# Attention weights transposed one step later, convolution taps moved beside the linear attention's values, and a scan's few-row products spread between matmuls

## The chip, the core and the metric

The kernel runs on one core of a Trainium2 chip. Five engines work side by side, each on its own in-order list of instructions, and meet at semaphores: TensorE (PE) for matrix products, VectorE (DVE), ScalarE (ACT), GpSimd (POOL), and SyncE (SP), which here issues the transfers of weights. The metric is the time of one execution in microseconds (us).

## What is computed

Two transformer blocks over 512 positions of width 1024, in float32. Only the parts that the change touches are shown.

```python
# block 1: three branches, gated, merged, then a feed-forward network
y_a = mla_branch(...)   # 8 heads, low-rank queries and keys, softmax attention
y_b = fox_branch(...)   # 8 heads, softmax attention with decay
y_c = ssm_branch(...)   # 16 heads, chunked state scan
# attention, by blocks of 128 queries
s = einsum('bqhd,bkhd->bhqk', q, k) * scale + mask
out = einsum('bhqk,bkhd->bqhd', softmax(s), v)
# block 2: spatial gating, gated linear attention, band attention (8 heads,
# with a bias), and a depthwise convolution of 31 taps with a layer norm
log_a = log_sigmoid(a_lr @ w_a2 + b_a) / 16
cum = cumsum(log_a)                      # in chunks of 64
k_dec = k * exp(total - cum); state = exp(total) * state + k_dec.T @ v
y = silu(layer_norm(depthwise_conv(glu, w[31])))
```

## The kernel before

**Precision.** A float32 product is made of three passes of a fast form: every operand is split into a high and a low part, and `product` (L393 to L395) issues high*high, low*high, high*low. A matmul of 128x128 by 512 columns appears on PE as one record.

**Weights.** All weights come as "slabs" of up to 1 MB through three buffers. For each slab SyncE issues the transfer, ScalarE writes its high part (`split`, L1124), VectorE the low part (`split`, L1623), and PE waits for that in `slab`. Where these two splits stand in the lists of ScalarE and VectorE is written by hand: `split(i)` makes all slabs up to number i. A slab of a gate (`gate_slab`) holds 256 output columns: two halves of 24 matmuls each, or four quarters of 12.

**Order.** The program is a list of stages (mla, fox, ssm, ..., convin, band, sgu, gla, gates2, ...). Four engines meet at the end of a stage (`boundary`); PE only reports there and goes on.

**Softmax attention** (`attention`, three times: tags mla, fox, band) runs over 16 steps, step j being one pair of heads and one block of queries t = j % 4, with t+1 blocks of keys. In a step PE makes the scores of both heads (L487), VectorE adds the mask and takes the row's bound (L1751), ScalarE takes the exponential in place and its sum (L1177), VectorE takes a reciprocal for each head (L1762) and scales the weights (L1763), PE transposes them (L498), ScalarE copies each head's transpose out of PSUM (L1188), PE multiplies them with the values (L511). PE transposes step j-2 (`LAG_T`) and multiplies step j-3 (`LAG_O`) behind the scores of step j; VectorE scales step j-1 behind the scores of step j. The first transposes of a stage have four extra matmuls before them (`keep_clock`, L388). In mla VectorE also splits one slab, right behind score 16.

**Scan** (`pe_ssm`, four tiles t of 128 positions). Few-row products `arow(q)` (L660) spread a row of running sums over the partitions: 16 rows of the array, four heads each. Between them stand the state products (L670, L677), the diagonal products (L688), transposes of finished rows (`yturn`, L643), and nine gate slabs (`SCAN_GATES`), two in each t and one behind. VectorE turns an `arow` into differences (`diff`, L2013), ScalarE into exponentials (`decay`, L1325), VectorE mixes them (`mix`, L2023), and the diagonal products wait for that.

**Depthwise convolution.** It is 124 "taps" on VectorE, each one instruction over 128x512 (L2338): 16 in convin, 60 beside the band's slabs, 8 inside the band's attention (one for every fourth score), 24 beside the slabs of sgu, and the last 16 at the end of sgu, ahead of the split for the slab "gasm". Behind them PE sums over channels (`column_sums`, L926: "cmean", later "cvar").

**Linear attention** (`pe_gla`). PE: slab gasm, cmean, two products with 16 rows ("la", L811, after a transfer of `gla_w_a2_2` that ScalarE issues at the stage's start, L1456), the values gv (two slabs), keys gqk 2 and 3, cvar, queries gqk 0 and 1, transposes of keys, gr. ScalarE makes the softplus of "la" in three steps and only then the high part of gv's second slab. VectorE then:

```python
split(slab_of["gasm", 0] + 1)
dve_conv_mean()
split(slab_of["gv", 0, 0])      # waits for ScalarE's high part
dve.wait_ge(soft_ready, 3)      # then softplus, and 16 cumulative scans
```

**Start of mla.** After the second of six low-rank columns both engines split slab 1 and VectorE builds the position tables (`dve_tables`), ScalarE their sines; the split of slab 2 comes behind.

## Time and profile before

| | us |
|---|---|
| median of 3 runs (2138.02 to 2139.4) | 2138.96 |
| the profiled execution | 2145.03 |
| its span on the core | 2143.3 |
| PE busy in the span | 2063.6 |
| VectorE busy | 1148.3 |
| ScalarE busy | 797.4 |

PE is busy for 96% of the span. The profiled execution is 6.07 us longer than the median run, 1.73 us of that outside its span. The trace lists, for each instruction, when it started, how long it took, and what ended the idle time before it. "PEclk" is the granted clock of TensorE: 1.00 is 2.4 GHz, 0.50 is 1.2 GHz.

### The profile page before, as it was taken

How to read it: one execution, taken by the hardware profiler on the slowest of the kernel's cores; microseconds unless marked ns; L12 is line 12 of the kernel's file. 1: busy time of each engine (PE TensorE's matmuls, PEld its weight loads, DVE VectorE, ACT ScalarE, POOL GpSimd, SP SyncE). 2: the span in 40 equal slices, each digit the busy share in tenths (PEclk: the TensorE clock that was granted, in tenths of full speed). 3: DMA queues.
4: the chain of work that ended last, by engine and by line, in shares of the span. 5: the costliest groups of instructions: out<-in, count | busy, mean ns of one | idle time of the engine just before them, and what ended most of it. 6: DMA issues, size and time to landing. Idle time of an engine off the chain costs nothing.

```text
span 2143.3 us, 23661 instructions
## 1 busy us (share of the span) xinstructions
PE 2063.6 (96%) x9677; PEld 1679.8 (78%) x9677; DVE 1148.3 (54%) x1706; ACT 797.4 (37%) x1116; POOL 28.3 (1%) x54
## 2 busy tenths in 40 slices
PE   7999999999999999999999899999999999999985
PEld 5886688878888788888878587888888788888874
DVE  5746637566434666366368884543435443234245
ACT  5536643344422433133232635342233333133132
POOL 0000000110000000000000000000000000000000
PEclk9999999999999999999999999999999999999998
DMA  4320023211333232332333122133232233333221
GB/s 126 99 79 21 1 79 99 79 59 59 118 99 98 79 99 98 98 93 84 100 117 99 41 89 79 59 99 99 98 97 86 76 97 98 98 99 98 98 90 58
DMA packets 164442, 184.45 MB, mean 86 GB/s; under 512 B 6759, under 2 KB 125798, under 8 KB 164334
## 3 DMA queue, kind: packets, MB, share of 16 engines
q1 hardware_dynamic: 160718, 173.98, 25.7%
q10 hardware_dynamic: 2912, 6.83, 0.9%
q0 software_dynamic: 704, 2.13, 0.3%
q8 instruction: 77, 1.26, 0.2%
q14 instruction: 31, 0.25, 0.0%
HBM read 180.81 MB, written 2.12 MB: 85 GB/s over the span
## 4 chain that ended last, share of the span: by engine, by line
PE 90%; DVE 6%; ACT 2%; issue 1%; DMA 0%; SPq 0%; POOL 0%; DVEq 0%; ACTq 0%; POOLq 0%
PE ps L393 27%; PE ps L395 26%; PE ps L394 26%; PE ps L487 2%; PE ps L511 1%; PE ps L498 1%; PE ps L468 1%; ACT arena L1149 1%; DVE WL L1623 1%; PE ps L660 1%; PE ps L688 1%; DVE arena L2338 1%; DVE arena L1713 0%; PE ps L670 0%; DVE X L2147 0%
## 5 line engine op out<-in xcount | busy, mean ns | idle before, releaser
L1623 DVE TENSOR_TENSOR WL<-W,WH 128x2048 fp32r<-128x2048 f32 (+1 forms) x166 | 375.4, 2261 | 382.6 <-ACT WH L1124 374.7
L393 PE MATMUL ps<-HH,WH 128*128 128x512 f32 x1400 | 550.1, 393 | 9.0 <-DVE HL L1646 4.6
L395 PE MATMUL ps<-HH,WL 128*128 128x512 f32 x1400 | 546.2, 390 | 0.0
L394 PE MATMUL ps<-HL,WH 128*128 128x512 f32 x1400 | 546.1, 390 | 0.0
L1124 ACT ACTIVATE WH<-W 128x2048 fp32r<-128x2048 f32 (+1 forms) x166 | 313.2, 1888 | 291.3 <-DMA W<-in_w_ff_dram 117.6
L393 PEld LDWEIGHTS ps<-HH,WH 128*128 128x128 f32 x1400 | 263.4, 188 | 67.5 <-issue 6.6
L395 PEld LDWEIGHTS ps<-HH,WL 128*128 128x128 f32 x1400 | 263.6, 188 | 55.3
L394 PEld LDWEIGHTS ps<-HL,WH 128*128 128x128 f32 x1400 | 263.7, 188 | 54.5 <-issue 0.7
L393 PE MATMUL ps<-WH,arena_r 128*128 128x512 f32 (+1 forms) x616 | 239.6, 389 | 2.8 <-issue 2.8
L395 PE MATMUL ps<-WH,arena_r 128*128 128x512 f32 (+1 forms) x616 | 239.2, 388 | 0.0
L394 PE MATMUL ps<-WL,arena_r 128*128 128x512 f32 (+1 forms) x616 | 239.0, 388 | 0.0
L393 PE MATMUL ps<-WH,HH 128*128 128x512 f32 x352 | 140.4, 399 | 5.6 <-DVE HL L1646 3.1
L394 PE MATMUL ps<-WL,HH 128*128 128x512 f32 x352 | 139.0, 395 | 0.0
L395 PE MATMUL ps<-WH,HL 128*128 128x512 f32 x352 | 139.0, 395 | 0.0
L393 PEld LDWEIGHTS ps<-WH,arena_r 128*128 128x128 f32 x616 | 116.2, 189 | 28.1 <-issue 5.2
L394 PEld LDWEIGHTS ps<-WL,arena_r 128*128 128x128 f32 x616 | 116.1, 189 | 23.1
L395 PEld LDWEIGHTS ps<-WH,arena_r 128*128 128x128 f32 x616 | 116.1, 188 | 23.0
L1384 ACT ACTIVATE arena<-ps,par 128x512 f32<-128x512 f32 x56 | 38.6, 689 | 209.1 <-PE ps L395 209.0
L2147 DVE TENSOR_TENSOR X<-X,ps 128x512 f32<-128x512 f32 x48 | 32.9, 685 | 100.2 <-PE ps L395 100.2
L393 PEld LDWEIGHTS ps<-WH,HH 128*128 128x128 f32 x352 | 67.4, 191 | 22.1 <-issue 8.3
L1435 ACT ACTIVATE arena<-ps 128x512 f32<-128x512 f32 x44 | 26.4, 599 | 155.4 <-PE ps L395 152.6
L2338 DVE SCALAR_TENSOR_TENSOR arena<-arena,par 128x512 f32<-128x512 f32 x120 | 81.1, 743 | 0.3 <-POOLq L1017 0.3
(328 smaller groups left out, 2257.6 us busy)
## 6 DMA issues: line engine op xcount, KB each, us to landing
W<-in_w_in_dram SPq DMA_DIRECT2D x50, 1024.0 KB, 5.1
W<-in_w_ff_dram SPq DMA_DIRECT2D x32, 1024.0 KB, 5.2
W<-in_ffn_w_up_dram SPq DMA_DIRECT2D x44, 512.0 KB, 4.6
W<-in_w_gate_dram SPq DMA_DIRECT2D x16, 1024.0 KB, 5.0
W<-in_ffn_w_down_dram SPq DMA_DIRECT2D x10, 1024.0 KB, 5.0
W<-in_w_out_dram SPq DMA_DIRECT2D x8, 1024.0 KB, 5.0
W<-in_w_branch_dram SPq DMA_DIRECT2D x8, 1024.0 KB, 5.0
W<-in_w_br_ssm_dram SPq DMA_DIRECT2D x4, 1024.0 KB, 5.0
```

The costliest lines, as they stand in the source:

```text
L393: pe.matmul(out_, st[0], mv[0], start=first, stop=False)
L394: pe.matmul(out_, st[0], mv[1], start=False, stop=False)
L395: return pe.matmul(out_, st[1], mv[0], start=False, stop=last)
L468: tr = pe.transpose(banks[k][:, t * P:(t + 1) * P], at(XN, NT, DM)[:, t, k * P:(k + 1) * P], ident[:, :])
L487: pe.matmul(b[:, 0:n], lhs(2 * pair + odd, t), rhs(2 * pair + odd, n), start=True, stop=True).then_inc(pe_done, 1)
L498: tr = pe.transpose(b[:, kb * P:(kb + 1) * P], p[:, r % 6, kb * P:(kb + 1) * P], ident[:, :])
L1124: act.activation(WH[:, j % RING, 0:n], W[:, j % RING, 0:n], ACT.Copy).then_inc(slab_hi, 1)
L1384: freed(act.activation(gate_tile(tag, i, c), b[:, :], ACT.Sigmoid, bias=pcol(bname, n * KT + cc * 4 + c)), ((tag, "g", n, cc), c))
L1435: freed(act.activation(raw[:, i % 2, c, 2:2 + S], b[:, :], ACT.Copy), (("up", i), c))
L1623: dve.tensor_tensor(WL[:, j % RING, 0:n], W[:, j % RING, 0:n], plain(WH[:, j % RING, 0:n]), ALU.subtract).then_inc(slab_lo, 1)
L2147: freed(dve.tensor_tensor(X[:, t, sl], X[:, t, sl], b[:, :], ALU.add), (tag, t, half))
L2338: ins = dve.scalar_tensor_tensor(y[:, c, :], glu[:, c, j:j + S], w, y[:, c, :], ALU.mult, ALU.add)
```

## The change

Six edits are made together.

1. `attention`, all three: `LAG_T` 2 to 3 and `LAG_O` 3 to 4. The weights lie in a buffer with a place for each t (`weights`), so they may live four steps. One reciprocal serves both heads, once both exponentials are there. For t of 0 and 1 both heads' transposes go to one bank and are copied at once.
2. Scan: `arow(0)` and `arow(1)` moved behind the state products, `arow(1)` between the halves of the gate slab; `arow(3)` and `yturn` between the halves of the second gate slab. VectorE's and ScalarE's lists follow.
3. Taps: none inside the band's attention, none at the end of sgu; 24 remain for gla, 8 of them right behind the split of gv's second slab, 16 behind the cumulative scans.
4. gla on PE: cmean behind gv instead of behind gasm, cvar behind both gqk slabs; VectorE's and ScalarE's parts of the convolution's norm follow. `cum` and `ke` move to other memory, since the taps' input still lives in the old place.
5. The transfer of `gla_w_a2_2` is issued at the start of sgu, with a semaphore of its own (`decay_in`).
6. Start of mla: slab 2 is split together with slab 1, before the tables.

The diff, with lines that only rename buffers left out:

```diff
@@ -48,7 +48,7 @@
     NB = 8
-    LAG_T, LAG_O = 2, 3
+    LAG_T, LAG_O = 3, 4
     PAIR_BANKS = (6, 7)
@@ -278,6 +279,22 @@
+def turned(s):
+    return s - s % 2 if s // 2 % NT < 2 else s
+def weights(p, s):
+    t = s // 2 % NT
+    at0 = t * (t + 1) * P + s % 2 * (t + 1) * P
+    return p[:, at0:at0 + (t + 1) * P]
+def turned_weights(pts, s):
+    n = (s // 2 % NT + 1) * P
+    at0 = s // 2 % 2 * 2 * S + s % 2 * n
+    return pts[:, at0:at0 + n]
@@ -322,7 +339,7 @@
 TAP_ORDER += [(j, c) for j in range(FIRST_TAPS, TAPS) for c in range(4)]
-TAPS_SLAB = 10
+TAPS_SLAB, LAST_TAPS = 10, 16
 BIAS = 14336
@@ -394,7 +411,7 @@
-    def gemm_f(name, w, kt, c0, tiles, src, n0=0):
+    def gemm_f(name, w, kt, c0, tiles, src, n0=0, between=None):
@@ -402,6 +419,8 @@
             mm.then_inc(pe_done, 1)
+            if between is not None and c == tiles // 2 - 1:
+                between()
@@ -490,27 +509,31 @@
                 for r in (2 * i, 2 * i + 1):
-                    b = bank((tag, "PT", r))
+                    if turned(r) == r:
+                        b, c = bank((tag, "PT", r)), 0
                     if r == 0:
...
                     for kb in range(t + 1):
-                        tr = pe.transpose(b[:, kb * P:(kb + 1) * P], p[:, r % 6, kb * P:(kb + 1) * P],
-                                          ident[:, :])
-                    tr.then_inc(pe_done, 1)
+                        tr = pe.transpose(b[:, (c + kb) * P:(c + kb + 1) * P],
+                                          weights(p, r)[:, kb * P:(kb + 1) * P], ident[:, :])
+                    c = t + 1
+                    if r == 2 * i + 1 or t >= 2:
+                        tr.then_inc(pe_done, 1)
             i = j - LAG_O
...
                     o = bank((tag, "O", pair), counted=False, pinned=PAIR_BANKS[pair % 2])
-                taken(pe, (tag, "PT", 2 * i))
-                taken(pe, (tag, "PT", 2 * i + 1))
+                taken(pe, (tag, "PT", turned(2 * i + 1)))
+                if t >= 2:
+                    taken(pe, (tag, "PT", 2 * i))
                 for kb in range(t + 1):
...
                                        v[:, kb, h * HD:(h + 1) * HD],
-                                       pts[:, (2 * i + odd) % 4, kb * P:(kb + 1) * P],
+                                       turned_weights(pts, 2 * i + odd)[:, kb * P:(kb + 1) * P],
                                        start=(kb == 0), stop=(kb == t))
@@ -661,8 +684,6 @@
-            arow(0)
-            arow(1)
             if t > 0:
@@ -676,8 +697,9 @@
                               start=True, stop=True).then_inc(pe_done, 1)
+            arow(0)
             for n, kind, cc, j in SCAN_GATES[2 * t]:
-                gate_slab("G1", n, kind, cc, j)
+                gate_slab("G1", n, kind, cc, j, lambda: arow(1))
             pe.wait_ge(xdt_ready, t + 1)
@@ -693,21 +715,23 @@
                     arow(2)
-                    arow(3)
+                    def small_products():
+                        arow(3)
+                        if t > 0:
+                            yturn(t - 1)
                     for n, kind, cc, j in SCAN_GATES[2 * t + 1]:
-                        gate_slab("G1", n, kind, cc, j)
-                    if t > 0:
-                        yturn(t - 1)
+                        gate_slab("G1", n, kind, cc, j, small_products)
         for n, kind, cc, j in SCAN_GATES[2 * NT]:
...
-    def gate_slab(tag, n, kind, cc, j):
+    def gate_slab(tag, n, kind, cc, j, between=None):
...
             w = slab(KT, 256, gate(2 * cc + j))
-            gemm_f((tag, "g", n, cc), w, KT, 0, 2, hn, 2 * j)
+            gemm_f((tag, "g", n, cc), w, KT, 0, 2, hn, 2 * j, between)
             slab_read()
@@ -716,10 +740,10 @@
             w = slab(kt, 512, krc(br, cc))
-            gemm_f((tag, "b", n, cc), w, kt, 0, 4, lambda k: [yh[:, k, :], yl[:, k, :]])
+            gemm_f((tag, "b", n, cc), w, kt, 0, 4, lambda k: [yh[:, k, :], yl[:, k, :]], 0, between)
         else:
             w = slab(kt, 256, krc(br, 2 * cc + j, 256))
-            gemm_f((tag, "b", n, cc), w, kt, 0, 2, lambda k: [yh[:, k, :], yl[:, k, :]], 2 * j)
+            gemm_f((tag, "b", n, cc), w, kt, 0, 2, lambda k: [yh[:, k, :], yl[:, k, :]], 2 * j, between)
         slab_read()
@@ -794,31 +818,31 @@
                   lambda h, n: KT_[part(h), h // 2, 0:n],
-                  at(12288, NT, 512), at(18432, 6, S), at(0, 4, S))
+                  at(12288, NT, 512), at(18432, 2560), at(0, 4 * S))
...
         slab_read()
-        pe.wait_ge(dve_taps, 4 * TAPS)
-        column_sums("cmean", at(CONV, 4, S))
         wa2, alr = at(25344, 256), at(22528, S)
-        pe.wait_ge(load_in, 16 * 5)
+        pe.wait_ge(decay_in, 16)
         taken(pe, ("gasm", 0))
...
         gemm_t_long("gv", full, 1536, hnt)
+        pe.wait_ge(dve_taps, 4 * TAPS)
+        column_sums("cmean", at(CONV, 4, S))
         w = slab(KT, 256, win(1280, 1536, "w_in_2"))
...
         slab_read()
-        pe.wait_ge(conv_squared, 4)
-        column_sums("cvar", at(18432, 4, S))
         w = slab(KT, 256, win(1024, 1280, "w_in_2"))
...
         slab_read()
+        pe.wait_ge(conv_squared, 4)
+        column_sums("cvar", at(18432, 4, S))
@@ -1171,21 +1195,25 @@
             if j < N // 2:
-                n = (j % NT + 1) * P
                 for s in (2 * j, 2 * j + 1):
                     taken(act, (tag, "S", s))
-                    act.activation(p[:, s % 6, 0:n], p[:, s % 6, 0:n], ACT.Exp, bias=rowneg[:, s:s + 1],
+                    act.activation(weights(p, s), weights(p, s), ACT.Exp, bias=rowneg[:, s:s + 1],
                                    scale=-1.0, accum_out=rowsum[:, s:s + 1]).then_inc(probs_ready, 1)
...
                 n = (i % NT + 1) * P
-                for r in (2 * i, 2 * i + 1):
-                    b = use(act, (tag, "PT", r))
-                    if i >= 2:
-                        act.wait_ge(pairs_out, N // 2 * nth + i - 1)
-                    freed(act.activation(pts[:, r % 4, 0:n], b[:, 0:n], ACT.Copy), (tag, "PT", r))
+                if i >= 2:
+                    act.wait_ge(pairs_out, N // 2 * nth + i - 1)
+                if i % NT < 2:
+                    b = use(act, (tag, "PT", 2 * i))
+                    both = pts[:, i % 2 * 2 * S:i % 2 * 2 * S + 2 * n]
+                    freed(act.activation(both, b[:, 0:2 * n], ACT.Copy), (tag, "PT", 2 * i))
+                else:
+                    for r in (2 * i, 2 * i + 1):
+                        b = use(act, (tag, "PT", r))
+                        freed(act.activation(turned_weights(pts, r), b[:, 0:n], ACT.Copy), (tag, "PT", r))
@@ -1200,7 +1228,7 @@
             if i == 1:
-                split(slab_of["c", 2])
+                split(slab_of["c", 2] + 1)
                 act.wait_ge(cos_arg, 1)
@@ -1338,9 +1366,9 @@
             decay(4 * t)
-            decay(4 * t + 1)
             if t > 0:
                 scale(t - 1)
+            decay(4 * t + 1)
             for n, kind, cc, j in SCAN_GATES[2 * t]:
@@ -1450,10 +1478,9 @@
             freed(act.activation(V[:, t, :], b[:, :], ACT.Copy), ("av", t, 0))
-        attention("band", 2, at(18432, 6, S), at(0, 4, S))
+        attention("band", 2, at(18432, 2560), at(0, 4 * S))
     def act_gla():
-        act.dma_start(at(25344, 256)[0:16, :], A["gla_w_a2_2"][0]).then_inc(load_in, 16)
         b = result(("gasm", 0))
@@ -1465,13 +1492,12 @@
         act.activation(la, la, ACT.Ln, bias=1.0).then_inc(soft_ready, 1)
+        v, r = at(14336, NT, 512), at(12288, NT, 512)
         split(slab_of["gv", 0, 0])
-        act_conv_squares()
-        v, r = at(14336, NT, 512), at(12288, NT, 512)
         for t in range(NT):
...
             freed(act.activation(v[:, t, :], b[:, :], ACT.Copy), ("gv", t, 0))
-        cum, ke = at(22528, 2, S), at(23552, 2, S)
+        cum, ke = at(2048, 2, S), at(3072, 2, S)
         act.wait_ge(decay_sums_ready, 1)
@@ -1479,22 +1505,22 @@
                        ACT.Exp).then_inc(decay_exps_ready, 1)
+        act_conv_squares()
         qz, kd = at(8192, 4, S), at(10240, 2, S)
...
             freed(act.activation(kd[:, c, :], b[:, :], ACT.Copy), ("gqk", 2 + c))
-        split(slab_of["gqk", 0] + 1)
-        taken(act, "cvar")
-        act.activation(at(11776, S), at(11776, S), ACT.Sqrt).then_inc(conv_root_ready, 1)
         for c in range(2):
...
             freed(ins, ("gqk", c))
+        split(slab_of["gr", 0, 0])
+        taken(act, "cvar")
+        act.activation(at(11776, S), at(11776, S), ACT.Sqrt).then_inc(conv_root_ready, 1)
         act_conv_out()
-        split(slab_of["gr", 0, 0])
         for t in range(NT):
@@ -1518,6 +1544,7 @@
     def act_sgu():
+        act.dma_start(at(25344, 256)[0:16, :], A["gla_w_a2_2"][0]).then_inc(decay_in, 16)
         act.dma_start(at(12288, 4, P), A["sg_w_2"][0].rearrange("g i j -> i g j")).then_inc(load_in, 16)
@@ -1746,9 +1773,9 @@
                     b = use(dve, (tag, "S", s))
-                    if s >= 6:
-                        use(dve, (tag, "PT", s - 6))
-                    freed(dve.tensor_tensor_reduce(out=p[:, s % 6, 0:n], in0=b[:, 0:n],
+                    if s >= 8:
+                        use(dve, (tag, "PT", turned(s - 8)))
+                    freed(dve.tensor_tensor_reduce(out=weights(p, s), in0=b[:, 0:n],
                                                    in1=mask(2 * pair + s % 2)[:, S - n:S],
@@ -1756,11 +1783,10 @@
             if 0 <= i < N // 2:
-                n = (i % NT + 1) * P
+                dve.wait_ge(probs_ready, base + 2 * i + 2)
+                link(dve.reciprocal(rowinv[:, 2 * i:2 * i + 2], rowsum[:, 2 * i:2 * i + 2]))
                 for s in (2 * i, 2 * i + 1):
-                    dve.wait_ge(probs_ready, base + s + 1)
-                    link(dve.reciprocal(rowinv[:, s:s + 1], rowsum[:, s:s + 1]))
-                    dve.tensor_scalar(p[:, s % 6, 0:n], p[:, s % 6, 0:n], rowinv[:, s:s + 1], None, ALU.mult)\
+                    dve.tensor_scalar(weights(p, s), weights(p, s), rowinv[:, s:s + 1], None, ALU.mult)\
                         .then_inc(weights_ready, 1)
@@ -1807,7 +1833,7 @@
             if i == 1:
-                split(slab_of["c", 2])
+                split(slab_of["c", 2] + 1)
                 dve_tables()
@@ -2026,7 +2052,6 @@
             diff(0)
-            diff(1)
             if t > 0:
@@ -2055,12 +2080,13 @@
             mix(0)
+            diff(1)
             mix(1)
...
             diff(2)
+            mix(2)
             diff(3)
-            mix(2)
             mix(3)
@@ -2188,17 +2214,13 @@
-        def beside_scores(s):
-            if s % 4 == 3:
-                taps(1)
-        attention("band", 2, at(18432, 6, S), lambda h: bias[:, h, :], at(4096, 4, S), beside_scores)
+        attention("band", 2, at(18432, 2560), lambda h: bias[:, h, :], at(4096, 4, S))
...
         dve.tensor_scalar(stat2[:, 0:2], pcol("gla_b", 0, 2), -1.0, None, ALU.mult).then_inc(gate_bias_ready, 1)
-        lv, la, cum, ke = at(20480, 2, S), at(21504, 2, S), at(22528, 2, S), at(23552, 2, S)
-        split(slab_of["gasm", 0] + 1)
-        dve_conv_mean()
+        lv, la, cum, ke = at(20480, 2, S), at(21504, 2, S), at(2048, 2, S), at(3072, 2, S)
         split(slab_of["gv", 0, 0])
+        taps(len(TAP_ORDER) - tapped[0] - LAST_TAPS)
         dve.wait_ge(soft_ready, 3)
@@ -2208,6 +2230,9 @@
         ins.then_inc(decay_sums_ready, 1)
+        taps(LAST_TAPS)
+        split(slab_of["gqk", 2])
+        dve_conv_mean()
         split(slab_of["gqk", 2] + 1)
@@ -2215,8 +2240,6 @@
         split(slab_of["gqk", 0] + 1)
-        dve_conv_norm()
-        split(slab_of["gr", 0, 0])
         kz = at(16384, NT, 2, 256)
@@ -2225,6 +2248,8 @@
             freed(ins, ("kd", c))
+        split(slab_of["gr", 0, 0])
+        dve_conv_norm()
         split(slab_of["gr", 0, 0] + 1)
@@ -2291,7 +2316,6 @@
         dve.tensor_tensor(v, v, bc(bb.unsqueeze(1), [P, NT, 512]), ALU.add).then_inc(sgu_values_ready, 1)
-        taps(len(TAP_ORDER) - tapped[0])
         split(slab_of["su", 3] + 1)
```

## Rows read from the trace of the kernel before

**Rows 1.** The page: the chain that ended last, by engine.

```profile
PE 90%; DVE 6%; ACT 2%; issue 1%; DMA 0%; SPq 0%; POOL 0%; DVEq 0%; ACTq 0%; POOLq 0%
```

**Rows 2.** Waits of PE: line, waited for, us in total, times, longest.

```profile
PE ps L498 <- DVE arena L1763: 8.7, 9, 1.7
...
PE ps L811 <- DMA arena<-in_gla_w_a_dram: 2.4, 1, 2.4
```

**Rows 3.** Timeline of ScalarE and PE, start of mla: start, us, instruction, [idle before].

```profile
42.21 1.90 ACT L1124 ACTIVATE WH<-W 128x2048 fp32r<-128x2048 f32 x1
...
46.55 0.50 PE L393 MATMUL ps<-HH,WH 128*128 128x512 f32 x1 [2.03 <-DVE WL L1623]
```

**Rows 4.** Windows: length, busy by engine, granted clock; scan five, then mla, band, gla.

```profile
437.50:440.90 3.40, 3.40 (x5) 1.35 (x4) 3.40 (x13) 3.34 (x6) 1.90 (x1) 0.50 0.02 5
...
512.60:515.90 3.30, 3.30 (x6) 1.45 (x5) 3.27 (x6) 1.50 (x3) 0.33 (x1) 0.50 0.00 0
185.00:188.20 3.20, 3.20 (x15) 2.06 (x14) 0.82 (x4) 1.51 (x5) 0.00 (x0) 0.50 0.01 3
1229.70:1232.90 3.20, 3.20 (x20) 2.49 (x19) 1.65 (x5) 1.06 (x3) 0.00 (x0) 0.52 0.00 0
1297.80:1304.40 6.60, 6.60 (x15) 4.34 (x14) 0.00 (x0) 5.80 (x6) 0.00 (x0) 0.50 0.00 0
```

**Rows 5.** Timeline of VectorE and PE, mla attention.

```profile
180.40 2.28 DVE L1623 TENSOR_TENSOR WL<-W,WH 128x2048 fp32r<-128x2048 f32 x1
...
183.64 1.22 PE L498 MATMUL ps<-ident,arena 128*128 128x128 f32 x8 [1.65 <-DVE arena L1763]
...
203.80 1.05 PE L498 MATMUL ps<-ident,arena 128*128 128x128 f32 x6 [0.61 <-DVE arena L1763]
```

**Rows 6.** Band attention: one pair's window, PE's waits, two of VectorE's groups.

```profile
1206.80:1216.95 10.15, 8.84 (x79) 5.39 (x78) 9.06 (x36) 7.37 (x24) 0.00 (x0) 1.00 0.00 0
...
PE ps L498 <- DVE arena L1763: 5.7, 5, 1.7
...
L2338 DVE SCALAR_TENSOR_TENSOR arena<-arena,par 128x512 f32<-128x512 f32 x6 | 4.5, 748 | 0.0
L1762 DVE RECIPROCAL rowinv<-rowsum 128x1 f32<-128x1 f32 x24 | 3.8, 156 | 0.0
```

**Rows 7.** Timeline of PE and VectorE in the scan, t = 2.

```profile
472.83 2.04 PE L660 MATMUL ps<-arena,ident 16*128 16x128 f32 x16
...
484.95 2.29 DVE L1623 TENSOR_TENSOR WL<-W,WH 128x2048 fp32r<-128x2048 f32 x1
493.96 2.16 DVE L2013 TENSOR_SCALAR arena<-ps,arena 128x128 f32<-128x128 f32 x8 [6.71 <-PE ps L660]
```

**Rows 8.** Timeline of VectorE and ScalarE, sgu's end and gla's start.

```profile
1272.85 10.69 DVE L2338 SCALAR_TENSOR_TENSOR arena<-arena,par 128x512 f32<-128x512 f32 x16
...
1305.43 1.90 ACT L1124 ACTIVATE WH<-W 128x2048 fp32r<-128x2048 f32 x1
...
1307.36 2.29 DVE L1623 TENSOR_TENSOR WL<-W,WH 128x2048 fp32r<-128x2048 f32 x1 [10.10 <-ACT WH L1124]
1309.57 1.22 DVE L2203 SCALAR_TENSOR_TENSOR arena<-arena 128x1024 f32<-128x1024 f32 x1
...
1311.55 3.02 DVE L2208 TENSOR_TENSOR_SCAN arena<-ones,arena 128x64 f32<-128x64 f32 x16
```

**Rows 9.** Timeline of PE in the same stretch, to the first transposed keys' use.

```profile
1284.72 0.50 PE L393 MATMUL ps<-HH,WH 128*128 128x512 f32 x1 [1.35 <-DVE WL L1623]
1290.34 3.59 PE L926 MATMUL ps<-arena,ones 128*128 128x512 f32 x8
1296.38 2.59 PE L811 MATMUL ps<-arena 16*128 16x512 f32 x4 [2.45 <-DMA arena<-in_gla_w_a_dram]
...
1323.37 0.39 PE L393 MATMUL ps<-HH,WH 128*128 128x512 f32 x1
...
1361.13 3.72 PE L839 MATMUL ps<-arena 128*128 128x256 f32 x16 [0.59 <-DVE arena L2226]
```

17 lines of the change are left out of this document (9 added, 8 removed).

## The prediction

> **What bounds the kernel now.** I read the page first. PE carries 90% of the chain that ended last, VectorE 6%, ScalarE 2% [rows 1]. So the time is PE's list of work, plus the places where PE waits, plus the stretches in which its matmuls run at half clock. An edit that only frees VectorE or ScalarE is worth what PE waits for them and no more.
>
> Second, the table of PE's waits. The one that the attention edit aims at is PE waiting for VectorE's scaled weights, 8.7 us in nine waits; the transfer that edit 5 aims at costs 2.4 us [rows 2]. Third, the granted clock in short windows. It fell to 0.50 (1.2 GHz) in five stretches of the scan, although PE is busy in all of each, in one stretch of the mla attention, in one near the end of the band attention, and for 6.6 us in gla [rows 4]. Work in a stretch of x us at half clock would take x/2 at full clock, so a stretch of 3.3 us costs about 1.65 us. Last, timelines of each place that the change touches.
>
> **Start of mla (edit 6).** PE waits 2.03 us for VectorE's low part of slab 2, whose high part ScalarE makes only at 42.21, behind the sine [rows 3]. The edit puts both splits ahead of the tables, where PE has two column tiles (24 matmuls each, which take 5.6 us in gasm [rows 9]) before it needs the slab. The tables move back by one split (2.29 us) plus a wait for ScalarE; nothing on PE waits for them here. Worth -2.0; bounds 0 (if the late tables delay the column sums behind them) and -2.0.
>
> **Attention (edit 1).** PE has the same matmuls. What changes is how long the weights of a step have: one whole step more, 2.6 us on average (a pair of heads, four steps, takes 10.15 us in band [rows 6]). Per pair VectorE has four reciprocals of 0.16 us fewer, ScalarE two copies fewer.
>
> - fox: PE is unbroken except for a wait of 0.61 us at the end, as in mla, where the row is 203.80 [rows 5], because the last weights are needed at once. Behind the last scores PE now has more left to do. -0.5.
> - mla: the same 0.61, and 1.65 us behind the slab that VectorE splits between two scores (2.28 us) [rows 5]. Then PE ran at half clock for 3.2 us, worth 1.6 [rows 4]. The extra step covers the late weights. But ScalarE's exponential of the next score waits for the same split, and ScalarE's copies are queued behind that exponential; so PE meets the lateness one step later, at the multiplication with the values. I take half of the wait away (-0.8) and half of the clock's cost (-0.8), since in band 1.3 us without PE work in a pair left the clock at 1.00 [rows 6] and one of 1.65 here did not. With the tail -2.2; bounds -0.6 and -3.9.
> - band: five waits, 5.7 us in all, for weights [rows 6]. They recur once a pair, after the longest step, where a tap of 0.75 us and two reciprocals stand between the score and the weights. Both causes go. The last wait is followed by a half-clock stretch of 3.2 us (0.52), worth 1.5 [rows 4]. New waits: at the start PE reaches its first multiplication having made four scores, and ScalarE's copy stands behind eight exponentials; I add 1.2 there, and 0.5 for copies in the rest. Sum -5.7 - 1.5 + 1.7 = -5.5; bounds -3 (the clock stays low, copies cost another 1 us) and -7.
>
> **Scan (edit 2).** No instruction is added or removed on PE. Its eight runs of 16 records of few-row matmuls (L660) take 2.04 us each; the timeline has each of the five half-clock stretches beginning within 1 us of the end of one, as the run that ends at 474.9 [rows 7]. Three runs had none behind them. The change cuts each run into two of 1.0 us with 5.6 us of dense work between them. Other work there (diagonal products, transposes) also fills the attentions, where the clock stayed up through unbroken pairs. So I expect the stretches to go: 16.6 us at 0.50 are worth 8.3. I leave one of the five, since a 16-row run now touches eight transposes, and take -6.8; bounds 0 and -8.3.
>
> What could eat it is VectorE's order. Now `diff(1)` comes behind the state updates, `mix(1)` behind that, and the split of the next gate slab behind `mix(1)`. Counting from the end of the last diagonal products at t = 2, with durations of this trace: rows' end, 3.6; `diff(0)` at 5.3 to 6.4; output and state updates (eight of 0.7) to 12; `mix(0)`, `diff(1)`, ScalarE's exponential, `mix(1)` to 15.1; ScalarE's high part to 16.3, the low part (2.29 [rows 7]) to 18.6. PE asks for the slab at 19.8. Slack 1.2 us; at t = 3 the same count leaves 0.3. I put the loss at 0.
>
> **sgu and gla (edits 3 to 5).** Four costs go:
> - 16 taps of 0.67 us no longer stand before the split of gasm's slab: the 1.35 us wait goes [rows 8, 9].
> - The 2.45 us wait for the transfer goes [rows 9]; in its place PE waits about 0.7 us for ScalarE's copy of gasm, which cmean used to cover.
> - The half-clock stretch of 6.6 us behind that wait [rows 4]: "la" has only 16 rows, so I let half of it stay (in "la" and the start of gv, where it does not delay VectorE and so is lost in the wait below).
> - The 0.59 us wait for the copies of transposed keys [rows 9].
>
> One cost comes, and it is the largest: PE now stands at cmean, behind gv, until the last tap. When is that? sgu ends on VectorE when its four outputs are done, some 3.8 us earlier than before; gasm's matmuls start at 1283.4 (1284.72 - 1.35) and end at 1289.0, "la" starts at 1289.65 instead of 1296.38 [rows 9], 6.7 us earlier. All that hangs on "la" moves with it. ScalarE's high part of gv's second slab, before at 1305.43 to 1307.3, ends at 1300.6; VectorE idled 10.10 us for it before [rows 8] and idles nearly as long after, because the taps stand behind that split, not before it. Then VectorE has: low part 2.29 (to 1302.9), 8 taps 5.35 (to 1308.2), softplus and scans 5.0 (from 1309.57 to 1314.57 before [rows 8]; to 1313.2), 16 taps 10.69 (to 1323.9). PE starts gv 2.6 us behind "la", at 1292.25. Before, gv took from 1298.97 to 1323.37, 24.4 us, with 5.4 us of it at half clock, so 21.7 at full; it would end at 1314.0. It idles 9.9 us. The work that it would hide under is at the front: VectorE's idle 10 us.
>
> Then cmean 3.6, and half clock after a wait this long, for 2 us of loss (the one after 2.45 us of waiting lasted 6.6 us, worth 3.3 [rows 4]). So the first gqk matmul comes at 1323.9 + 3.6 + 2.0 = 1329.5, against 1323.37 before [rows 9]: +6.1. Behind it cvar and the norm have more time than before, and -0.6 for the keys' copies: +5.5. Bounds +3 (no half clock, and the chain of "la" 0.8 us quicker) and +8.
>
> Here a rule of the Trainium skill was weighed. The trace shows half clock in the scan with no idle time on PE. The Trainium skill ("TensorE: Matmul & The Clock Gate", section "HAM oscillation") blames idle gaps of the matrix engine for the loss of clock; by that the scan's stretches are not the few-row products' doing, and the edit would bring nothing there. The trace disagrees in that there was no gap. The same page (section "Part 4: PE-mode transpose") says that transposes do not count as busy; by that a run of `arow(3)` with `yturn` is as bad as before. The attentions, nearly a third of whose work is transposes, kept the clock up here.
>
> **The sum**: -2.0 - 2.2 - 0.5 - 5.5 - 6.8 + 5.5 = -11.5 us. The profiled execution took 2145.03, 6.07 above the median of the runs. The differences are taken over to the median: 2138.96 - 11.5 = **2127.5**.
>
> **The rivals.**
> - *The clock in the scan does not come back* (it falls around any group of small products, wherever it stands). For: PE was busy there throughout, so no idle gap explains it. Against: the runs of 2.04 us beside the stretches. +6.8: 2134.3. The Trainium skill's rule on idle gaps, above, would give this.
> - *The extra lag brings nothing*: PE waits for ScalarE's copies instead of VectorE's weights, once a pair. For: ScalarE's list in a step is serial, exponentials first. Against: it is busy 7.37 of 10.15 us a pair in band [rows 6]. Band and mla give up their 7.7: 2135.2.
> - *The taps hide after all*: VectorE is done before gv ends. It would need 10 us more before the split. +5.5 becomes about -6.4: 2115.6. Only a list that runs otherwise than I read would do this.
> - *Slower: the gate slabs come late.* If VectorE's chain in the scan is longer than counted and each of seven gate slabs in the loop finds its low part a whole split (2.29 us) late, PE loses 16.0: 2143.5. It decides from 1.7 us a slab on (11.5 / 7), that is 2.9 us beyond my count at t = 2. Speaking for it: VectorE waits for `arow(1)` in the middle; against: the count has no item that I could not read.
>
> **How the numbers follow.** The forecast (2121 to 2132) 0.60; the clock does not return 0.13; the lag brings nothing 0.10; taps hide 0.05; late slabs 0.08; the rest, several small misses, 0.04. The best of all bounds together is -2.0 - 3.9 - 0.6 - 7 - 8.3 + 3 = -18.8, or 2120.2; the range goes a little below it for the hidden taps, and above to the two rivals at 2134 to 2135 with some 2 us: 2118 to 2137. A difference under 0.2% (4.3 us) is no more than a measurement of this kernel can tell from none. Faster means under 2134.7, slower over 2143.2: the forecast, the taps, and half of the two middle rivals (0.60 + 0.05 + 0.12, and 0.01 of the rest) give 0.78 faster; 0.14 the same; 0.08 slower.
>
> **What would show it.** In the profile after: no wait of PE near 46.5; no wait for weights in band, some 1 us for copies at its start; the clock at 1.00 through the scan in all but one place; no wait before gasm or for a transfer; one wait of PE at the column sums behind gv, 8 to 10.5 us, released by a tap, and VectorE idle for some 9 us ahead of gv's second low part. The prediction is wrong if that wait is missing or doubled by clock, if the scan has waits for low parts, or if half clock stays around its small products.

## The result, and the profile after

The changed kernel takes **2127.53 us** (median of nine runs, 2126.11 to 2135.53), beside 2138.83 for the kernel before in the same session: a ratio of 0.9944, 95% interval 0.9929 to 0.9959, that is -12.0 us (-8.8 to -15.2). The forecast was 2127.5.

The profiled execution took 2127.42 us with a span of 2125.7; that of before took 2145.03. So the two traces differ by 17.6 us and the medians by 11.3, and the first task is to see which part of the 17.6 belongs to the change. Windows between the same instructions of both kernels tell. First the kernel before, in the stretches of mla attention, scan, and band to sgu's first transposes, and then of everything from gla's end to the embedding's first transposes, where nothing was changed (columns as in [rows 4]):

```profile
160.84:208.87 48.03, 44.78 (x309) 29.46 (x308) 33.71 (x133) 34.40 (x100) 0.00 (x0) 0.96 0.07 23
402.65:556.20 153.55, 153.55 (x761) 124.46 (x759) 98.50 (x165) 67.14 (x74) 9.97 (x5) 0.94 0.20 62
1191.26:1257.40 66.14, 59.80 (x405) 41.58 (x406) 56.73 (x166) 37.78 (x103) 0.00 (x0) 0.97 0.16 49
1405.07:2087.76 682.69, 671.08 (x2962) 555.26 (x2961) 267.41 (x271) 207.44 (x226) 0.00 (x0) 0.99 0.29 95
```

The same stretches of the changed kernel, then its two half-clock places (band, gla), which answer to [rows 4]:

```profile
156.74:201.68 44.94, 41.42 (x310) 28.69 (x309) 31.38 (x117) 33.74 (x92) 0.00 (x0) 1.00 0.08 25
393.46:542.00 148.54, 148.54 (x761) 119.64 (x759) 97.03 (x165) 67.28 (x74) 9.48 (x5) 1.00 0.20 64
1176.06:1238.37 62.31, 58.34 (x404) 41.60 (x405) 49.08 (x142) 36.92 (x95) 0.00 (x0) 0.97 0.17 52
1391.45:2070.48 679.03, 667.02 (x2961) 551.96 (x2960) 267.31 (x271) 207.52 (x226) 0.00 (x0) 0.99 0.30 96
...
1183.50:1187.00 3.50, 3.50 (x22) 2.21 (x18) 1.93 (x9) 2.33 (x9) 0.00 (x0) 0.54 0.01 2
1299.50:1309.80 10.30, 5.17 (x7) 2.24 (x8) 7.27 (x9) 1.59 (x8) 0.00 (x0) 0.51 0.01 2
```

The fourth row of each is the lesson in reading a single pair of traces: the same instructions, no edit, and 3.7 us less, because in this execution less time at half clock followed the waits of the norms there, 6.8 us of it where before had 17.1. By the starts of the same instructions on PE, the stretches that the change touches and the rest come to:

| stretch (us on PE) | before | after | difference | forecast |
|---|---|---|---|---|
| start of mla, the wait alone | 2.03 | 0 | -2.0 | -2.0 |
| mla attention | 48.03 | 44.94 | -3.1 | -2.2 |
| fox attention, to the sums behind z | 90.6 | 88.6 | -2.0 | -0.5 |
| scan | 153.55 | 148.54 | -5.0 | -6.8 |
| band attention and its end | 66.14 | 62.31 | -3.8 | -5.5 |
| sgu and gla, to the updates | 103.7 | 109.3 | +5.5 | +5.5 |
| all changed stretches | | | -10.4 | -11.5 |
| everything else (half clock that fell otherwise) | | | -7.2 | 0 |

-10.4 for the changed stretches agrees with the medians' -11.3. The last row need not be the change's doing: in the fourteen profiled kernels of this document, the stretch from gla's end to the embedding takes 677.2 to 682.9 us with the same instructions, with 3.4 to 17.1 us of half clock, and both ends of that range come from kernels with all six edits. In the table of PE's waits of the changed kernel, what answers to [rows 2] is this; L518 stands where L498 stood, L534 is the multiplication with the values:

```profile
PE ps L950 <- DVE arena L2362: 9.5, 1, 9.5
...
PE ps L534 <- ACT arena L1212: 6.2, 8, 2.1
...
PE ps L410 <- DVE WL L1650: 1.5, 1, 1.5
```

The 8.7 us for VectorE's scaled weights are gone and 6.2 us for ScalarE's copies have come; the 2.4 us for the transfer and the waits for low parts ahead of slab 2 of mla and of gasm are gone; and one wait of 9.5 us for a tap has come, at cmean (L950). PE's share of the chain that ended last went from 90% [rows 1] to 91%, ScalarE's from 2% to 3%:

```profile
PE 91%; DVE 5%; ACT 3%; issue 1%; DMA 0%; SPq 0%; POOL 0%; DVEq 0%; POOLq 0%
```

The band attention in the timeline of PE, the rows with a wait; they answer to the waits of [rows 6]:

```profile
1183.16 0.63 PE L534 MATMUL ps<-arena 128*64 128x128 f32 x4 [2.06 <-ACT arena L1212]
1193.58 0.44 PE L534 MATMUL ps<-arena 128*64 128x128 f32 x4 [0.29 <-ACT arena L1212]
1202.48 0.44 PE L534 MATMUL ps<-arena 128*64 128x128 f32 x4 [0.30 <-ACT arena L1212]
1211.38 0.44 PE L534 MATMUL ps<-arena 128*64 128x128 f32 x4 [0.72 <-ACT arena L1212]
```

One step of the pipeline still ends late in every pair, but it is ScalarE's copy, queued behind exponentials. The largest comes at the start, and the half-clock window at 1183.5 above lies behind it.

And gla's start on VectorE and PE, which answers to [rows 8, 9]:

```profile
1281.47 2.29 DVE L1650 TENSOR_TENSOR WL<-W,WH 128x2048 fp32r<-128x2048 f32 x1 [9.59 <-ACT WH L1148]
1283.68 5.39 DVE L2362 SCALAR_TENSOR_TENSOR arena<-arena,par 128x512 f32<-128x512 f32 x8
...
1290.97 3.02 DVE L2230 TENSOR_TENSOR_SCAN arena<-ones,arena 128x64 f32<-128x64 f32 x16
1293.91 10.66 DVE L2362 SCALAR_TENSOR_TENSOR arena<-arena,par 128x512 f32<-128x512 f32 x16
...
1304.62 6.14 PE L950 MATMUL ps<-arena,ones 128*128 128x512 f32 x8 [9.53 <-DVE arena L2362]
1310.20 0.79 PE L410 MATMUL ps<-HH,WH 128*128 128x512 f32 x1
```

VectorE idles 9.59 us for ScalarE's high part, with 24 taps still to do, and a little later PE idles 9.53 us for the last of these taps.

### The profile page after: what moved, and what is told of

It reads as the page before. It is cut to its first block, busy times and chain, and to the rows that moved or that the text cites. A ratio compares the mean times of both kernels' runs of the same rounds, so it can differ in the third digit from the quotient of the medians.

```text
span 2125.7 us, 23510 instructions
## 1 busy us (share of the span) xinstructions
PE 2043.7 (96%) x9677; PEld 1666.8 (78%) x9677; DVE 1140.8 (54%) x1658; ACT 795.9 (37%) x1092; POOL 28.4 (1%) x54
## 4 chain that ended last, share of the span: by engine, by line
PE 91%; DVE 5%; ACT 3%; issue 1%; DMA 0%; SPq 0%; POOL 0%; DVEq 0%; POOLq 0%
PE ps L410 27%; PE ps L412 27%; PE ps L411 27%; PE ps L506 2%; PE ps L534 1%; PE ps L518 1%; ACT arena L1173 1%; PE ps L487 1%; PE ps L683 1%; DVE arena L2362 1%; PE ps L710 1%; DVE X L2173 0%; ACT arena L1200 0%; DVE arena L1740 0%; PE ps L950 0%
```

## Experiments

Every ratio is against the kernel before, run on the same chip in the same session. Length and clock of a stretch are from the one profiled execution of each kernel.

### One edit at a time

**Edit 2 alone** (scan), in the kernel before.

> The kernel before with edit 2 alone. Theory (the clock was lost behind the unbroken runs of 16 few-row matmuls, and putting dense matmuls between them has a price of its own): all five half-clock stretches of the scan go, worth 8.5 us, and the switching between small and dense matmuls gives 3.5 back, so the scan takes some 149 us instead of 154 and the kernel 2133.8 us (-5). Rival 1 (the stretches went for another reason, such as the other state of buffers and slabs that the rest of the change brings): stretches still there, switching paid for, 2142. Rival 2 (switching costs nothing and the 3.5 us came from elsewhere): 2130.3.

Measured: 2135.48 us, ratio 0.9971 (0.9955 to 0.9987), -6.2 us. The scan's window:

```profile
399.94:548.49 148.55, 148.55 (x761) 119.64 (x759) 97.09 (x165) 67.28 (x74) 9.48 (x5) 1.00 0.21 64
```

148.55 us at clock 1.00, to a hundredth what the changed kernel has. The edit does this by itself. Rivals 1 and 2 fall by the trace; the runs' interval alone (-2.8 to -9.6) would still hold rival 2.

**Edit 1 alone** (attention), the taps left inside band.

> The kernel before with edit 1 alone; the eight taps stay inside the band attention. Theory (the extra step of lag is what shortens the attentions): mla -3.1, fox -2.0, band -3 to -4 as in the changed kernel, 2130.5 us. Rival 1 (in band the gain needs the taps gone): band keeps about half of its waits for weights, 2132.5. Rival 2 (the lag brings nothing, and what mla and band gained came from the other edits): 2138.

Measured: 2129.66 us, ratio 0.9947 (0.9931 to 0.9962), -11.3 us. From band's first scores to sgu's first transposes, and the scan, which this kernel did not change:

```profile
1184.07:1245.41 61.34, 57.17 (x404) 40.72 (x405) 53.84 (x150) 37.24 (x95) 0.00 (x0) 1.00 0.17 52
```

```profile
393.38:551.50 158.12, 158.12 (x760) 128.01 (x759) 98.55 (x165) 67.12 (x74) 10.03 (x5) 0.91 0.19 60
```

mla took 44.94 as in the changed kernel, and band 61.34 at full clock, so edit 1 brings the gain with the taps in place; both rivals fall. No run separates its parts: the longer lag, the one reciprocal for two heads, and the one bank and copy for t of 0 and 1. The kernel with edits 1, 2 and 6 (`a_nogla`, below) has the taps in band and one half-clock stretch there and takes 62.85, against 62.31 of the changed kernel with one too: taking the taps out was worth 0.5 us. The scan is a second result: with the same instructions as in [rows 7], half clock came behind seven places here (27 us in all) instead of five, and took 4.6 us longer.

**Edits 3 to 5 undone**, in the changed kernel.

> The changed kernel with edits 3 to 5 undone: eight taps inside band's attention, the rest at the end of sgu, cmean behind gasm, the transfer in gla. Theory (these edits cost what the stretch from sgu's start to the updates lost): 2127.5 - 5.4 = 2122.1 us, less up to 1 that the taps cost in band. Rival (what they cost there comes back behind gla, by earlier low parts): 2127.5.

Measured: 2124.75 us, ratio 0.9926 (0.9910 to 0.9942), -15.8 against the kernel before, where the changed kernel has -12.0. Edits 3 to 5 cost some 4 us by the runs' ratios, whose intervals overlap, and 5.5 in the trace. The rival (what they cost comes back behind gla) falls by the traces alone. There the stretch from gla's end to the embedding took 682.86 us in this kernel and 679.03 in the changed one, but the difference goes with half clock (17.1 against 6.8 us) and not with the edits: `a_taps16` below, which has all of them, took 682.84.

**Edit 5 alone** (the transfer issued earlier), in the kernel before.

> The kernel before with edit 5 alone (the transfer of the decay's weights issued at the start of sgu). Theory 1 (the half clock behind la follows from PE's wait of 2.45 us for the transfer): the wait and the 6.8 us of half clock both go, -2.4 - 3.3 = -5.7 us of 2138.8: 2133.1. Theory 2 (the half clock follows from la's 16-row matmuls, as in the scan): only the wait goes, half clock stays, 2136.4. Rival (VectorE's low part of gv's second slab is what gv waits for in the end, so PE waits there instead): 2138.8.

Measured: 2136.55 us, ratio 0.9986 (0.9973 to 0.9999), -3.0 us, and in the profile no wait at la. Its stretch from la to the transposed keys:

```profile
1289.44:1338.48 49.04, 49.04 (x206) 38.28 (x206) 24.95 (x35) 28.36 (x43) 2.61 (x2) 1.00 0.23 74
```

49.04 us at clock 1.00, where the kernel before took 52.20 with 6.6 us at 0.50 [rows 4]. In this trace theory 1 holds: without PE's idle 2.45 us la's 16-row products were not followed by half clock. The runs' interval (-0.2 to -5.8) holds the -5.7 as its end only. The other profiles leave theory 2 open in part. All six kernels with the transfer in gla have half clock behind la, 3.4 to 6.8 us of it after a wait of 1.96 to 2.48 us. But of the seven in which PE waits only 0.8 us for the copy of gasm, four have it too, 3.4 us each (`a_copyfirst`, `a_best1`, `a_best2`, `a_best3`), and three have none (the changed kernel, `a_run16`, `a_taps16`). In `a_copyfirst` the granted clock is 0.50 from 1269.4 to 1272.8 us, right behind this:

```profile
1266.87 1.95 PE L833 MATMUL ps<-arena 16*128 16x512 f32 x4 [0.81 <-issue]
```

So the wait of 2 us is not the only condition there. `b_dma`, the one kernel without any half clock or wait there, has cmean directly ahead of la.

**Edit 6 alone** (slab 2 split ahead of the tables).

> The kernel before with edit 6 alone (slab 2 split ahead of the tables). Theory: PE's wait of 2.03 us for that low part goes and no other comes: from the first transposes to the mla attention 2.0 us less, apart from half clock. Rival (the late tables delay what stands behind them): a new wait of 0.5 to 2 us near 55 us for the column sums or the norm.

Run once, for the trace (2141.19 us): PE's waits between 30 and 60 us are only the 0.7 for ScalarE that stood there before, and the mla attention starts 2.3 us earlier. The late tables cost nothing. This kernel's mla attention happened to run at full clock:

```profile
158.53:204.94 46.41, 43.16 (x310) 28.50 (x309) 33.74 (x133) 34.34 (x100) 0.00 (x0) 1.00 0.07 24
```

46.41 against 48.03 is what half clock cost there (1.6), and 46.41 against 44.94 what edit 1 saves (1.5).

### The taps in VectorE's idle time

```diff
-TAPS_SLAB, LAST_TAPS = 10, 16
+TAPS_SLAB, LAST_TAPS = 10, 8
-                split(slab_of["gv", 0, 0])
                 taps(len(TAP_ORDER) - tapped[0] - LAST_TAPS)
+                split(slab_of["gv", 0, 0])
```

> The changed kernel with 16 of the 24 taps ahead of VectorE's low part of gv's second slab, and 8 behind the cumulative scans. Theory (VectorE stood idle for 9.6 us ahead of that low part and PE waited 9.5 us for the last tap, so the idle time takes the taps): the low part comes 1.1 us late at most, PE's wait at cmean shrinks to under 1 us, the half-clock stretch of 10 us behind it (worth 5) goes or shrinks to 3: 2127.5 - 9 - 4 = 2114.5 us. Rival 1 (the wait moves to gv's second slab, since the low part is then late by the taps): only 2 to 4 us gained, 2124. Rival 2 (the half clock has another cause, the 16-row matmuls of la): wait gone, half clock stays, 2118.5.

Measured: 2117.52 us, ratio 0.9888 (0.9872 to 0.9905). VectorE's timeline there, and the window from la to the transposed keys:

```profile
1269.45 10.69 DVE L2362 SCALAR_TENSOR_TENSOR arena<-arena,par 128x512 f32<-128x512 f32 x16
1280.77 2.29 DVE L1650 TENSOR_TENSOR WL<-W,WH 128x2048 fp32r<-128x2048 f32 x1 [0.62 <-ACT WH L1148]
...
1287.90 5.36 DVE L2362 SCALAR_TENSOR_TENSOR arena<-arena,par 128x512 f32<-128x512 f32 x8
```

```profile
1270.40:1322.83 52.43, 52.43 (x213) 39.77 (x213) 33.38 (x53) 29.62 (x45) 2.51 (x2) 1.00 0.29 94
```

The idle of 9.59 us is 0.62, the low part starts no later, PE's wait at cmean is gone and with it the half clock: 52.43 us instead of 64.72. The 12.3 us are the wait (9.5) and what half clock took from cmean, 6.14 instead of 3.59 (2.6). Both rivals fall. The edit as a whole is worth having; in the changed kernel the taps stood on the wrong side of one split.

### ScalarE's copies ahead of its exponentials

On top of that, in the kernel of `a_taps16`, the block of `attention` on ScalarE that copies step j-3's turned weights is put in front of the block with step j's exponentials.

> The changed kernel with the taps as in a_taps16, and ScalarE's copies of a step's turned weights ahead of the exponentials of the newest step. Theory (PE's waits for those copies, 6.5 us in nine, come from copies that stand behind exponentials): they shrink to under 2 us and the half clock in band goes: 2117.5 - 4.5 - 1.5 = 2111.5 us. Rival (the exponentials come late instead, so that VectorE's weights come late): new waits for weights, 2117 to 2121.

Measured: 2112.49 us (2110.67 to 2113.19), ratio 0.9878 (0.9860 to 0.9897). Its band and mla:

```profile
1176.38:1234.12 57.74, 57.11 (x405) 40.91 (x406) 48.90 (x142) 36.99 (x95) 0.00 (x0) 1.00 0.19 56
160.17:202.25 42.08, 41.35 (x309) 28.55 (x308) 31.01 (x117) 33.10 (x92) 0.00 (x0) 1.00 0.09 26
```

The table of PE's waits has no row for copies any more, and for weights only the 0.2 us of band that was there before. Band is 4.6 us shorter than in the changed kernel, mla 2.9. The rival falls: the exponentials do not make the weights late. The gain rests on the traces and on medians from two chips (5.0 us under `a_taps16`); the ratios, 0.9878 and 0.9888, do not separate the two kernels.

### What the clock in the scan hangs on

`a_run16`: the runs of 16 whole again, but the first of a tile behind the state products and the transposes between halves.

```diff
                     arow(0)
+                    arow(1)
-                        gate_slab("G1", n, kind, cc, j, lambda: arow(1))
+                        gate_slab("G1", n, kind, cc, j)
...
                             arow(2)
+                            arow(3)
                             def small_products():
-                                arow(3)
                                 if t > 0:
                                     yturn(t - 1)
```

> The changed kernel with the scan's few-row products back in unbroken runs of 16 on PE (arow(0) with arow(1), arow(2) with arow(3)); the runs stay behind the state products, and only the transposes stay between the halves. Theory (a run of 16 is what the clock is lost behind, not its place): half clock behind most of the eight runs, 17 to 27 us of it, while the switches cost some 1.5 us less than in the changed kernel: scan 154 to 159 us instead of 148.5, kernel 2127.5 + 6 to 9 = 2134 to 2137. Rival 1 (the order around the runs was the cause, the run touching the column products of the state): no half clock, scan 147, kernel 2126. Rival 2 (the transposes between the halves keep the price of switching): no half clock, 148.5.

Measured: 2127.43 us, ratio 0.9948 (0.9931 to 0.9965). The theory, and with it the prediction's reading of [rows 7], falls in its first half: with all eight runs of 16 in place there is one half-clock stretch, not five, and the scan takes 146.98 us, next to rival 1's 147. So I looked at what stands around them. In `b_attn`, PE's timeline ahead of the half clock that begins at 504.1:

```profile
499.54 1.04 PE L663 MATMUL ps<-ident,arena 128*128 128x128 f32 x8
500.42 1.90 PE L708 MATMUL ps<-arena 128*128 128x64 f32 x16
502.15 0.66 PE L672 MATMUL ps<-arena 128*128 128x128 f32 x4
502.74 2.42 PE L680 MATMUL ps<-arena,ident 16*128 16x128 f32 x16
505.09 1.22 PE L690 MATMUL ps<-arena 128*128 128x512 f32 x1
```

Transposes, diagonal products, cb and the few-row products follow each other for 5.5 us. `b_order` changes only that, in the kernel before (PE's list is shown; `diff`, `mix` and `decay` follow on VectorE and ScalarE as in edit 2):

```diff
-                    arow(0)
-                    arow(1)
                     if t > 0:
                         taken(pe, ("up", t - 1, 1))
...
+                    arow(0)
+                    arow(1)
                     for n, kind, cc, j in SCAN_GATES[2 * t]:
```

> The kernel before with one part of edit 2: arow(0) and arow(1) behind the state products, both runs of 16 whole, nothing set between halves of a gate slab, the transposes behind the slab as before. Theory A (what counts is how long the small products of any kind follow each other on PE: in the kernel before, transposes, diagonal products, cb and arow make 5.3 us together at t = 2 and 3, 4.4 at t = 1, and diagonal products with arow 3.9 in four places): the longest stretches fall to 3.7, half clock remains behind at most two places of 3.9 (0 to 7 us of it), scan 146 to 149 instead of 153.5, kernel 2132 to 2134. Theory B (the run of 16 few-row matmuls itself): five to eight half-clock stretches as before, scan 153.5, 2139. Rival (the diagonal products wait for arow's results, which now come later): a wait of PE of up to 1 us before each, scan over 150.

Measured: 2135.37 us, ratio 0.9965 (0.9940 to 0.9990). The scan, and the same place of PE's timeline:

```profile
402.46:549.32 146.86, 146.86 (x760) 120.85 (x759) 97.16 (x165) 67.27 (x74) 9.47 (x5) 0.99 0.21 65
```

```profile
466.19 1.03 PE L643 MATMUL ps<-ident,arena 128*128 128x128 f32 x8
467.06 1.90 PE L688 MATMUL ps<-arena 128*128 128x64 f32 x16
468.79 0.66 PE L652 MATMUL ps<-arena 128*128 128x128 f32 x4
469.29 1.88 PE L668 MATMUL ps<-arena 128*128 128x512 f32 x4
471.01 1.88 PE L675 MATMUL ps<-arena 128*128 128x512 f32 x4
472.82 2.04 PE L660 MATMUL ps<-arena,ident 16*128 16x128 f32 x16
```

Without a wait in the scan, moving two lines of PE's list made the scan 6.7 us shorter in this trace, and the kernel by 7.5 us (2.1 to 12.8) in the runs. Theory B falls: no run of 16 with dense matmuls on both sides was followed by half clock. Theory A is borne out in that, but not in its order by length. Counting the places in every profile, by PE's timeline and the granted clock behind it:

| what follows each other on PE | us | followed by half clock |
|---|---|---|
| (transposes,) diagonal products, cb, run of 16; four kernels with the old order | 4.4 to 5.5 | 9 of 12 places |
| diagonal products, run of 16; the same four kernels | 3.9 | 11 of 16 |
| the same; `a_run16`, `b_order`, `a_best1` | 3.9 | 4 of 12 |
| run of 16 between dense matmuls; these three, `a_best3` | 2.0 | 0 of 16 |
| all places of the changed kernel, `b_scan`, `a_nogla`, `a_taps16`, `a_copyfirst`, `a_best2`, `a_best3` | up to 3.1 | 0 |

`b_dma`, whose scan is that of the kernel before, had its half clock behind three places of 3.9 us and behind none of the longer ones. So a long stretch of small products opens the door and something else, which no run here separates, decides whether the clock falls. Why the places of 3.9 us were hit less often once the others were gone is open too; with these counts it may be chance.

`a_best1` and `a_best2` put this into the kernel of `a_copyfirst`; `a_best1` has the scan of `a_run16`, `a_best2` sets `arow(2)` and `arow(3)` both between halves.

> The kernel of a_copyfirst with the scan of a_run16. Theory (each switch between dense and small matmuls has a price, and eight of them go): scan 145.4 us without half clock, 147 with one stretch, against 148.5: 2112.5 - 1.5 to 3 = 2110.3. Rival (half clock comes back as often as it is spared): 2112 to 2114.

> As a_best1, but arow(2) and arow(3) stand between the halves of the second gate slab with the transposes, so that no small products follow the first diagonal products: the longest stretch of small products that remains is 3.1 us. Theory A: no half clock in the scan in any run, scan 145.5, 2109.5. Rival (VectorE makes its mixes too late, since only half a slab lies between them and the diagonal products): PE waits 1 to 3 us at each t, scan 150 to 156, 2113 to 2120.

Measured: `a_best1` 2116.37 us, ratio 0.9881 (0.9859 to 0.9904), scan 150.09 with 10 us at half clock: its rival's reading, though the time lies above its range too. `a_best2` 2118.04 us, ratio 0.9899 (0.9879 to 0.9920). Its scan is at full clock, but PE waits 2.7 us for VectorE:

```profile
PE ps L410 <- DVE arena L2096: 1.3, 1, 1.3
PE ps L410 <- DVE WL L1651: 1.2, 1, 1.2
```

The second is a gate slab whose low part comes late, the wait of the prediction's slower rival: this order brings it about, the changed kernel's does not. Only 1.6 and 1.2 us of what the two lose against `a_copyfirst` (3.9 and 5.5 by the medians) lie in the scan; in their profiles the unchanged stretch behind gla is 5.5 and 5.7 us longer, with 13.7 us more at half clock.

`a_best3` keeps `arow(3)` between the halves and only makes the first run whole again:

```diff
                     arow(0)
+                    arow(1)
-                        gate_slab("G1", n, kind, cc, j, lambda: arow(1))
+                        gate_slab("G1", n, kind, cc, j)
```

> The kernel of a_copyfirst with arow(0) and arow(1) together behind the state products (a whole run of 16 with dense matmuls on both sides), and arow(3) with the transposes between the halves as in the changed kernel. Theory (half clock needs a longer unbroken stretch of small products than 2.9 us, and every insertion between the halves of a slab costs some 0.4 us): no half clock in the scan, and 148.5 less four insertions, 146.9 to 147.3 us; the kernel 1.4 us under the 2112.5 of a_copyfirst, 2111. Rival (a run of 16 is enough by itself wherever it stands): half clock behind two or more of the four runs, scan 148.5 to 150, 2113.

Measured: 2113.27 us (2108.5 to 2116.86), ratio 0.9869 (0.9844 to 0.9893), and the scan:

```profile
392.17:539.06 146.89, 146.89 (x760) 119.71 (x759) 96.97 (x165) 67.16 (x74) 9.47 (x5) 1.00 0.21 65
```

1.64 us less than the 148.53 of `a_copyfirst`, with four insertions fewer and no half clock in either: 0.41 us for one insertion of a run of 8 between the halves of a slab. The rival falls in this trace. The runs don't separate `a_best3` from `a_copyfirst`; both are some 14 to 16 us faster than the changed kernel (0.9869 and 0.9878 against 0.9944).

## Why the prediction was right, and which of its terms were not

**The sum** held to 1 us in the changed stretches, and the forecast of 2127.5 met 2127.53. Part of this is luck: the scan and band brought 3.5 us less than forecast, mla and fox 2.4 more, and nothing in the prediction made them cancel.

**Start of mla**: right, -2.0, and nothing waits for the tables (`b_mla`).

**mla**: -3.1 against -2.2. The half clock went wholly (-1.6); I had let half of it stay. The waits brought nothing, where I had -0.8 and -0.6: 2.4 us for weights went, and 2.7 us for ScalarE's copies came, by the mechanism that I gave, PE one step later at the multiplication with the values:

```profile
165.44 0.44 PE L534 MATMUL ps<-arena 128*64 128x128 f32 x4 [1.46 <-ACT arena L1212]
178.74 0.66 PE L534 MATMUL ps<-arena 128*64 128x128 f32 x8 [1.06 <-ACT arena L1212]
```

The other 1.5 us lie in what counts as PE's busy time, in all three attentions, and the prediction had no term for them; fox shows them best.

**fox**: -2.0 against -0.5. From its first scores to the sums behind z, without half clock in either, `b_scan` took 87.25 us and `b_attn` 85.71. 

```profile
219.28:306.53 87.25, 86.16 (x500) 64.72 (x501) 45.65 (x149) 49.83 (x121) 0.56 (x2) 1.00 0.12 37
```

```profile
214.25:299.96 85.71, 84.78 (x501) 64.77 (x501) 43.21 (x133) 49.24 (x113) 0.57 (x2) 1.00 0.12 38
```

PE is not busy for 1.1 us in the one and 0.9 in the other, so listed waits account for 0.2 of the 1.5 us. Most of the rest is in the transposes. The same 80, each with a record as long, cover 0.9 us less; first `b_scan`, then `b_attn`:

```profile
L500 PE MATMUL ps<-ident,arena 128*128 128x128 f32 x80 | 12.4, 276 | 0.7 <-DVE arena L1766 0.6
...
L515 PE MATMUL ps<-ident,arena 128*128 128x128 f32 x80 | 11.5, 275 | 0.0
```

In `b_scan` PE pauses between the two heads of a step, in each step with t = 2 and in the last one, and starts to load the second head's weights just after VectorE has scaled them (226.36 + 0.42 = 226.78):

```profile
226.36 0.42 DVE L1766 TENSOR_SCALAR arena<-arena,rowinv 128x384 f32<-128x384 f32 x1
...
226.90 0.31 PEld L500 LDWEIGHTS ps<-ident,arena 128*128 128x128 f32 x3 [0.22 <-issue]
```

The pause of 0.22 us is shorter than a transpose's record (276 ns), so PE counts as busy through it and no table of waits names VectorE; in `b_attn` it is gone. So edit 1 removed waits for weights that the prediction could not read off the table of waits. At full clock the transposes fell in the same way in mla (12.7 in `b_mla` to 11.5) and in band (13.5 in `b_order` to 12.2). What the other 0.4 us of fox are stays open.

**band**: -3.8 against -5.5. Mis-sized terms: the first wait for copies is 2.06 us where I had put 1.2, the later ones 1.3 together instead of 0.5, and the half clock, forecast to go (-1.5), moved from the last wait to the first. That would leave -2.3; the shorter busy time, for which I had no term, gave 1.5 back. ScalarE's order was the cause (`a_copyfirst`), as the second rival had it, though for a part of the gain only.

**Scan**: -5.0 against -6.8. The step that failed is "No instruction is added or removed on PE", taken to mean that the edit costs nothing there. All five stretches went, one more than forecast, but each insertion costs 0.41 us (`a_best3`), 3.3 us for the eight of them. Of the half clock's price the forecast had 0.50 us per us; 153.55 against 146.86, with 17.1 against 3.4 us of it, gives 0.49. The reading that the runs of 16 by themselves cost the clock was wrong too (0 of 16 between dense matmuls), without harm to the number. VectorE's count held: no gate slab was late in the changed kernel.

The trace of before had spoken against a rule, and for the scan the runs settle it. The scan's half clock comes with PE busy in all of each stretch, and goes when dense matmuls are set between the small ones. The Trainium skill ("TensorE: Matmul & The Clock Gate", section "HAM oscillation") names idle gaps of the matrix engine as what loses the clock; by that the scan edit would have brought nothing. The scan doesn't agree. In gla the trace agrees for the wait of 9.5 us: the clock fell within it and was full when it went (`a_taps16`). For the wait of 2.45 us it agrees in part: the half clock was gone in `b_dma`, but four kernels have some behind a wait of only 0.8 us there.

**sgu and gla**: +5.5 against +5.5, nearly by its own steps: gasm without its wait (1.35 to 0), the wait for the copy of gasm 0.81 (0.7), VectorE's idle 9.59 ("nearly as long" as 10.10), PE's wait 9.53 (9.9), half clock in cmean 2.6 (2.0). Behind la the half clock went wholly, where I had left half of it; it would have vanished in PE's wait either way.

**The rivals.** The clock came back, edit 1 brought most of what it should, the slabs were in time. The taps did not hide, and could have: the prediction's sentence that it "would need 10 us more before the split" was a description of the edit that `a_taps16` makes.

## What to carry to other kernels

When an engine idles ahead of one instruction and another engine later waits for the first one's backlog, move the backlog in front of that instruction before anything else: here it was worth 10 us. Work that is queued behind newer work on a serial engine (copies behind exponentials) can undo a deeper pipeline; put the older step's work first. Small matmuls are cheap to move next to dense ones and dear to cut into pieces: change the order of whole runs first, and split only what still stands too long in a row.

Compare traces stretch by stretch. Here 7 of the 17.6 us between two profiled executions lay where nothing had been changed.

## What the runs showed of the hardware

- Half clock without an idle gap: five stretches in the scan before, 27 us of it in the same instructions in `b_attn`, none in the changed scan. The clock is not lost at the same places in kernels with the same code there, so a gain from it must be read over several kernels or runs.
- Half clock costs about half of its length: 13.7 us more of it made the scan 6.7 us longer.
- A run of eight 16-row matmuls set between the halves of a slab's dense ones, instead of next to another such run, costs 0.41 us (1.64 us for four).
- A wait shorter than the matmul record before it shows as busy time: 80 transposes covered 12.4 us with such pauses and 11.5 without.
- One idle wait of 9.5 us of PE was followed by matmuls at half clock, 6.14 us for eight that take 3.59. Behind four 16-row matmuls, half clock came in six of six profiles after a wait of 1.96 to 2.48 us, in four of seven after 0.8 us, and not in the one without a wait.
